# A two-layer encoder kernel: the expert tables multiplied as plain f32, and 96 of 256 tokens gathered instead of 32

## The reference

```python
def peer_ffn(h, w_q, sub_keys, u_tab, v_tab):
    q = rms_norm((hb @ w_q).reshape(PEER_BLOCK, PEER_HEADS, 2, PEER_D_KEY // 2))
    s = jnp.einsum('thpd,hpkd->thpk', q, sub_keys)            # 2 x 128 sub-keys per head
    v_top, i_top = lax.top_k(s, PEER_TOPK)                    # 16 best of each half
    best_s, best_pos = lax.top_k(cand_s, PEER_TOPK)           # 16 best pairs, 8 heads
    gate = jax.nn.softmax(best_s, axis=-1)
    u = jnp.take(u_tab, idx, axis=0)
    act = jax.nn.gelu(jnp.einsum('td,thkd->thk', hb, u))
    v = jnp.take(v_tab, idx, axis=0)
    return jnp.einsum('thk,thkd->td', gate * act, v)
```

## Time and profile before

| | |
|---|---|
| median of 3 runs | 1838.51 us (1835.72 to 1839.15) |
| profiled execution, first to last instruction (span) | 1830.5 us |
| around the span (median less span) | 8.0 us |
| PE busy | 1796.4 us, 98% |
| DVE busy | 1476.1 us, 81% |
| ACT busy | 1115.6 us, 61% |
| POOL busy | 769.2 us, 42% |
| moved by DMA | 391.70 MB, mean 214 GB/s |

### The profile page before, as it was taken

How to read it: one execution, slowest core, us unless ns; L and a number is a source line. 1 busy time by engine, 2 the same in 40 slices (tenths; PEclk the granted TensorE clock), 3 DMA queues, 4 the chain that set the end, 5 groups by cost and what they waited for, 6 DMA issues and landing times. The chain is left out here.

```text
span 1830.5 us, 38340 instructions
## 1 busy us (share of the span) xinstructions
PE 1796.4 (98%) x11836; PEld 1695.5 (93%) x11836; DVE 1476.1 (81%) x3273; ACT 1115.6 (61%) x2184; POOL 769.2 (42%) x452
## 2 busy tenths in 40 slices
PE   8999999999999999999999999999999999999998
PEld 6889999999999999999978899999999999999998
DVE  4765888988887888888667568889888878888886
ACT  5765566667776555555567555666677765555554
POOL 6545320037766444343064462100476755444430
PEclk9999999999999999999999999999999999999999
DMA  8232266664444899999512323666644448888884
GB/s 319 93 137 94 70 209 206 206 217 154 156 149 152 310 384 387 353 380 365 170 62 93 138 93 108 209 203 206 208 158 149 156 167 336 338 321 321 333 299 148
DMA packets 105485, 391.70 MB, mean 214 GB/s; under 512 B 12288, under 2 KB 16000, under 8 KB 102976
## 3 DMA queue, kind: packets, MB, share of 16 engines
q1 hardware_dynamic: 86336, 322.57, 50.6%
q0 software_dynamic: 19072, 68.23, 9.7%
HBM read 388.86 MB, written 1.05 MB: 213 GB/s over the span
## 5 line engine op out<-in xcount | busy, mean ns | idle before, releaser
L630 PE MATMUL ps<-fhl,wh 128*128 128x448 f32 (+1 forms) x2560 | 542.4, 356 | 4.3 <-DVE ps L1606 4.3
L630 PE MATMUL ps<-ghl,wh 128*128 128x448 f32 x2048 | 462.6, 367 | 1.7 <-DVE wl L1841 0.9
L630 PEld LDWEIGHTS ps<-fhl,wh 128*128 128x128 f32 x2560 | 429.7, 189 | 31.7 <-issue 3.4
L630 PEld LDWEIGHTS ps<-ghl,wh 128*128 128x128 f32 x2048 | 366.3, 189 | 26.3 <-issue 1.3
L1192 ACT ACTIVATE wh<-nat 128x1024 fp32r<-128x1024 f32 x260 | 275.7, 1060 | 177.2 <-PE ps L630 91.6
L1841 DVE TENSOR_TENSOR wl<-nat,wh 128x1024 fp32r<-128x1024 f32 x252 | 307.9, 1222 | 74.2 <-ACT wh L1320 73.7
L611 POOL TENSOR_TENSOR wl<-nat,wh 128x1024 fp32r<-128x1024 f32 x112 | 268.6, 2398 | 115.8 <-ACT wh L1192 115.8
L630 PEld LDWEIGHTS ps<-fhl,wl 128*128 128x128 f32 x2304 | 300.5, 191 | 9.0 <-POOL wl L580 1.0
L630 PE MATMUL ps<-fhl,wl 128*128 128x224 f32 (+1 forms) x2304 | 303.6, 274 | 0.6 <-POOL wl L580 0.6
L1319 ACT ACTIVATE ghl<-grid 128x224 fp32r (+1 forms) x252 | 98.6, 391 | 300.8 <-PE ps L630 287.0
L630 PEld LDWEIGHTS ps<-ghl,wl 128*128 128x128 f32 x2048 | 269.5, 191 | 6.5
(11 more groups left out here) (206 smaller groups left out, 2238.9 us busy)
## 6 DMA issues: line engine op xcount, KB each, us to landing
nat<-in_peer_u SPq DMA_DIRECT2D x256, 512.0 KB
nat<-in_peer_v SPq DMA_DIRECT2D x256, 512.0 KB
grid<-in_peer_wq SPq DMA_DIRECT2D x8, 2048.0 KB, 10.7
grid<-in_w_out SPq DMA_DIRECT2D x2, 4096.0 KB, 12.7
grid<-in_w_in SPq DMA_DIRECT2D x3, 2048.0 KB, 16.0
grid<-in_w_in SPq DMA_DIRECT2D x24, 256.0 KB
grid<-in_bias SPq DMA_DIRECT2D x2, 1664.0 KB, 16.8
grid<-in_w_in SPq DMA_DIRECT2D x2, 1024.0 KB, 23.5
```

What stands on the lines that cost most here:

```text
L630: return nc.tensor.matmul(dst, a, b, start=first, stop=last)
```

## The change

Three things change together.

- **No split in U and V.** `wh`, `wl`, `ghl` and all that makes them are gone from the two stages (they stay in the projections and queries). Each block is multiplied as it lands, plain f32, 8 products of 160 columns. `nat` is joined by `ring`, so that the stream has 8 slots; they are freed by PE itself (`prod_done`, `y_done`).
- **96 tokens gathered (NS = 96, DT = 160), one a partition.** A gather brings 96 rows of 4 KB, one pick of each of 96 tokens. That makes 128 gathers of U rows and 128 of V rows a layer, with 8 buffers. `dot` and `add_row` work on 96 partitions x 1024. The sums need no small product: DVE adds them to `x`.
- **Fewer gates.** 40 groups of four tokens, one beside every second block of the last 80 of U. ACT makes three of four `hota` by two steps each, DVE one.

```diff
-NS = 32
+OCT = 8
+NO = NK // OCT
+NS = 96
 DT = SEQ - NS
-NP = 4
-NPK = PH * TOPK // NP
-QS = (1, 15, 28)
-NB = DT // 4
+NPK = PH * TOPK
+GT = 4
+NG4 = DT // GT
+NB = 2 * NG4
 NA = NK - NB
+EARLY_DOTS = 24
...
-    for s in range(QUAD):
-        sp.wait_ge(rest_pool, past[rest_pool] + 2 * (NB + s - 1 - QUAD))
+    for s in range(OCT):
+        sp.wait_ge(prod_done, past[prod_done] + (NK - OCT + s + 1))
         fetch_v(0, s)
...
     def gather(m):
-        b, rows = m % 3, u_rows if m < NPK else v_rows
-        if m >= 3:
-            pool.wait_ge(gath_used, past[gath_used] + m - 2)
-        nc.gpsimd.indirect_dma_start(gath[b], None, rows, bass.IndirectOffsetOnAxis(
-            ap=picks[:, 1, m % NPK:m % NPK + 1].bitcast(U32), axis=0)).then_inc(gath_in[b], 16)
+        if m >= OCT:
+            pool.wait_ge(gath_used, past[gath_used] + m - OCT + 1)
+        nc.gpsimd.indirect_dma_start(gath[m % OCT][own, :], None, u_rows if m < NPK else v_rows, bass.IndirectOffsetOnAxis(
+            ap=lists[own, 3, m % NPK:m % NPK + 1].bitcast(U32), axis=0)).then_inc(gath_in[m % OCT], 16)
     pool.wait_ge(picked, past[picked] + 2)
...
+    for m in range(2 * NPK):
+        gather(m)
...
-    def product(q, s, rest, before):
-        pe.wait_ge(summed, past[summed] + count + 1)
-        pe.wait_ge(high_ready, past[high_ready] + count * 2 + 2)
+    def product(q, s):
+        pe.wait_ge(nat_in[s], past[nat_in[s]] + q * 16 + 16)
+        if not isinstance(q, int) or q * OCT + s >= 4:
+            pe.wait_ge(act_stored, past[act_stored] + q * OCT + (s - 3))
         for k in range(KD):
-            ins = mm(both, wh[:, b, k * P:(k + 1) * P], fhl[:, :, k, 0:DT], k == 0, False)
-        ins.then_inc(high_used, 1)
-        pe.wait_ge(rest, past[rest] + count * 2 + (2 - 2 * before))
-        for k in range(KD):
-            ins = mm(ps[:, 4 + b, 0:DT], wl[:, b, k * P:(k + 1) * P], fh[:, k, 0:DT], False, k == KD - 1)
+            ins = mm(ps[:, UBANKS[s % 4], 0:DT], slots[s][:, k * P:(k + 1) * P], xf[:, k, :], k == 0, k == KD - 1)
         ins.then_inc(prod_done, 1)
...
+    def late_oct(q):
+        for s in range(OCT):
+            product(q, s)
+            if s % 2 == 0:
+                gates(q - QA, s // 2)
...
     def block_v(q, s):
-        need_high(q, s)
-        for k in range(KD):
-            high_y(s % 2, k)
-        need_rest(q, s)
+        pe.wait_ge(nat_in[s], past[nat_in[s]] + q * 16 + 16 * (NO + 1))
         for k in range(KD):
-            ins = rest_y(s % 2, k)
+            ins = mm(block_y(k), slots[s][:, k * P:(k + 1) * P], at(grid8, q, s), first and k % 2 == 0, last and k % 2 == 1)
         ins.then_inc(y_done, 1)
...
+    def dot(n):
+        dve.wait_ge(gath_in[b], past[gath_in[b]] + 16 * (n // OCT + 1))
+        v.tensor_tensor_reduce(out=gath[b][own, :], in0=gath[b][own, :], in1=xs[own, :], scale=1.0, scalar=0.0,
+                               op0=ALU.mult, op1=ALU.add, accum_out=dots[own, n:n + 1]).then_inc(gath_used, 1)
+    for n in (*range(20), *range(31, 47), 64, 65, *range(20, 31), *range(47, 63)):
+        routing(n)
...
+    for m in range(NG4):
+        times_gates(m)
+        if m + 2 < NG4:
+            hots(m + 2)
+        for i in range(2):
+            dot(EARLY_DOTS + 2 * m + i)
+            times_gelu(NA + 2 * m + i, m + 1)
+    for n in range(EARLY_DOTS + 2 * NG4, NPK):
+        dot(n)
+    dve.wait_ge(acts_ready, past[acts_ready] + 1)
+    ch.step(v.tensor_tensor(amount[own, :], acts[own, :], lists[own, 0, 0:NPK], ALU.mult))
+    for n in range(NPK):
+        add_row(n)
+    dve.wait_ge(gath_used, past[gath_used] + 2 * NPK)
+    ch.step(v.tensor_tensor(x[own, 0, :], x[own, 0, :], acc[own, :], ALU.add))
```

More of the change, by code:

```diff
@@ L1323, in _ @@
-                    with act.Fori(1, QS[1]) as q:
-                        for s in range(QUAD):
-                            block_v(q, s)
+                    loop(act, 3, QA - 1, early_oct)
+                    act.wait_ge(lists_t, past[lists_t] + 1)
+                    A(ikt[:, :], ps[:, 6, 0:SEQ], ACT.Copy)
+                    A(jkt[:, :], ps[:, 6, SEQ:], ACT.Copy)
+                    A(nwkt[:, :], ps[:, 7, 0:SEQ], ACT.Copy, scale=-1.0)
+                    A(wkt[:, :], ps[:, 7, 0:SEQ], ACT.Copy).then_inc(listt_ready, 1)
@@ L1326, in _ @@
+                    act.wait_ge(listt_ready, past[listt_ready] + 1)
+                    for s in range(OCT):
+                        gelu(QA - 1, s)
+                        if s in (2, 5):
+                            hot_i(0, s // 3)
+                    late_oct(QA)
+                    loop(act, QA + 1, NO - 1, late_oct)
+                    late_oct(NO - 1)
                     act.wait_ge(gath_used, past[gath_used] + NPK)
-                    A(acts, dots, ACT.Gelu_apprx_tanh).then_inc(acts_ready, 1)
@@ L1328, in _ @@
-                    with act.Fori(QS[1], NQ) as q:
-                        for s in range(QUAD):
-                            block_v(q, s)
+                    A(acts[own, :], dots[own, :], ACT.Gelu_apprx_tanh).then_inc(acts_ready, 1)
                     if l == DEPTH - 1:
-                        low_sums(past[y_chunk], past[y_done])
+                        turn_y(past[y_chunk])
             @block.vector
@@ L1808, in quad_g @@
-                    def quad_g(g, first=False, last=False):
-                        for s in range(QUAD - last):
-                            if s:
-                                times_gelu(g, s - 1)
-                            elif not first:
-                                times_gelu(g, QUAD - 1, 1)
-                            add_halves(g + QA, s, half_b, s % 2)
-                            times_gates(g, s, first and s == 0)
-                            if not (last and s >= 2):
-                                hots(g + (s + 2) // QUAD, (s + 2) % QUAD, iota_ps)
@@ new lines, in _ @@
+                    for n in (*range(20), *range(31, 47), 64, 65, *range(20, 31), *range(47, 63)):
+                        routing(n)
+                    dve.wait_ge(picked, past[picked] + 2)
+                    for n in range(4):
+                        dot(n)
+                    routing(63)
+                    for n in range(4, EARLY_DOTS // 2 + 2):
+                        dot(n)
+                    ch.before()
+                    dve.wait_ge(listt_ready, past[listt_ready] + 1)
+                    hots(0)
@@ new lines, in _ @@
+                    hots(1)
+                    for n in range(EARLY_DOTS // 2 + 2, EARLY_DOTS):
+                        dot(n)
+                    dve.wait_ge(ones_ready, past[ones_ready] + late.shape[1])
+                    dve.wait_ge(act_stored, past[act_stored] + NA)
+                    for m in range(NG4):
[5 more added lines that the diff above has]
+                            times_gelu(NA + 2 * m + i, m + 1)
```

610 lines of the change are left out of this document (193 added, 417 removed).

## The result

The changed kernel takes **2105.7 us** (median of four runs, 2104.95 to 2123.99) where the kernel before, measured beside it, takes 1837.1 (1834.27 to 1839.15): a ratio of 1.1495, 95% interval 1.145 to 1.154. The forecast was 1740 and faster. It is 15% slower, and outside every case that the prediction listed.

What follows compares the result with a forecast made beforehand. PE was to bound U and DMA to bound V: 212.1 + 319 + 350 + 204.2 + 319 + 320 + 7.5 = 1731.8 us of span, with 8.0 to the median 1740 us. Its own range was 1715 to 1770, with rivals 1690 to 1843.

Steps and rivals of the forecast that it cites:

- the DMA term: Gathers and stream in U and V: at 386 GB/s U holds its pace, V is DMA-bound at 350 and 320 us.
- I take equal halves of 386: V: gathers and stream each get 193 GB/s, so the 144 gathers left take 293 us.
- 1.835 MB, 349 GB/s: under 386. So U holds its pace: Late part of U: two gathers and two blocks per 5.26 us of PE fit within the DMA rate.
- when 24 dots more (30 us) are done as well: U: gates begin at block 48, at 105 us, with 24 more dots by DVE already done.
- slower than before: Rival, V: only 12 engines carry 96-row gathers, 145 GB/s, 2.72 us each; 1858 us, 1.1% slower; 10% chance.
- the ports' case: Rival with 12% chance, most of it (10) counted as faster; its claim is not in the text given.
- the 84% for faster: Whole kernel: summed chance of a gain above 0.2% (3.7 us), from the forecast's 50% and parts of the rivals.
- a pass of 135 ns (136.5): PE in U and V: a 160-column pass takes 136.5 ns, so a block of 16 passes takes 2.18 us.
- DVE and POOL not the bound: DVE's group in U, 4.8 to 4.9 us, fits PE's 5.26; POOL costs nothing in V; POOL as bound 10%, 1820 us.
- both waiting for transfers in V: V: PE waits for transfers into `nat` and `ring`, about 0.5 us a block, and DVE waits for gathers.
- the border of 204: Between the layers, from V's end to the next U: left as it was, 204.2 us.
- a cost left out: V, where PE now pauses: a granted clock below 1 would cost time that the sum did not count.

Runs made afterwards that it cites:

- 1: Small kernel of transfers alone, encoder work left out: stream, gathers and plain transfers, alone or mixed; 96-row gathers 254 GB/s, 283 beside a 128-row stream.
- 6: Gathers alone, 16 KB rows, few kept of 128, 96 or 64 places, other work left out; fifth stretch: rows 0-3, 32 and 33 of 96, 27 GB/s.
- 3: Changed kernel with 128-row gathers, three for every four picks, the fourth pick reusing the third's rows, same gathered bytes: 1718.85 us, 0.936 of before.
- 7: Changed kernel with gathers of 128 places, every fourth skipped by an out-of-bounds index, tokens moved to the other partitions: 1735.0 us, 0.946 of before.
- 2: Changed kernel with all 128 rows in every gather, including rows nobody reads: 1819.53 us, 0.991 of before.

## Why the prediction was wrong

- **The step that failed:** the DMA term. "I take equal halves of 386" in V, and "1.835 MB, 349 GB/s: under 386. So U holds its pace" in U. The 386 came from stretches in which all transfers had 128 rows. A 96-row gather is another shape, and it does not only go slowly itself, it takes the stream's rate down with it: 283 GB/s in the mix (1), 272 to 309 in the kernel. The halves were right, the 386 was not. I carried a rate measured on one shape over to another, with a range of 375 to 400 around it.
- **The same terms with the measured rate.** V of layer 1: 144 gathers at 2.76 us are 397 us, and the last one is issued at 2048.3 us, 49 us before the end, in which the last gathers land and PE does the last 18 blocks. U of layer 1: the 80 blocks with gates need 1.835 MB per group, at 299 GB/s 6.1 us instead of 5.26, 35 us over 40 groups. The trace has them at 261 us instead of 214, so 12 us more. Here a second step failed, "when 24 dots more (30 us) are done as well": at the first of these blocks only 16 of the 24 were done, since VectorE waited for gathers, and 8 gathers (3.1 MB, 10 us at this rate) fell into the late part too. Behind these late dots PE also waited once for a one-hot (line 1594), 5 us a layer. The first 48 blocks took 110 us where 105 was forecast. The main part of the miss of U and of V has one cause.
- **The rivals.** In time "slower than before" (10%, 1858 us) came nearest, 248 us under the measurement. No run shows the term of the ports' case (12%, of which 10 are in the 84% for faster). In its place the runs showed that 96 rows laid evenly over both halves of the partitions are no faster (48 and 48 rows, 224 GB/s against 253), and that two engines with rows in 0-3, 32 and 33 together get the rate of one (27 GB/s, 6). That this is the whole price of a 96-row transfer is argued, not shown. No case had gathers and stream together as slow as 283 GB/s (1), so the range ended at 1843, 263 us under the measurement.
- **Right:** a pass of 135 ns (136.5); DVE and POOL not the bound; the equal halves, which no row of before showed (205 and 205 in 3; 142 and 147 in V of the changed kernel); both waiting for transfers in V; the border of 204. With the shape mended the time comes near the forecast of 1740, at 1719 (3) and 1735 (7), but partly by luck, since DMA moved 406 to 410 GB/s there and not 386: in 7 that offsets the turns lost to skipped places, and V of layer 1 is 284 us to its last product and a tail of 34, where 320 without a tail was forecast.
- **The clock.** It was granted at 0.77 in 640 to 700 with PE busy 38.8 of 60 us, and at 1.00 in 1800 to 1900 with 67.5 of 100. V is bound by gathers there, 2.63 us apart, so PE's slower passes were covered; I did not test that apart. The prediction had named this as a cost left out; with DMA mended little of it returns (mean clock 0.984 in 7 and 0.994 in 3, 0.965 after).
- **Slips in the sum, none of which decides it:** PE alone comes by the prediction's own terms to 1621 + 8 us, not 1590 + 8. With about 6 MB of weights the stream brings 104 blocks and not 102, and V of layer 0 is some 345 us, not 350. The 8.0 us around the span compare one execution's span with the median of others; in the profiled executions here time and span differ by 1.8 us.
- **Open:** how 64 and 112 rows are dealt (of 64 rows, 0 to 3 had packets of 1228 ns, while 0, 16, 32 and 48 had 611), and how much of the loss at 96 rows (254 GB/s against 389 to 399) is two engines slowing each other as in the fifth stretch of 6. The three parts of the change were not tried apart: what dropping the split gives with 32 gathered tokens no run shows.

## What to carry to other kernels

A DMA rate belongs to a shape: before you change how many partitions a transfer writes, measure the new shape alone and beside the stream, because a full DMA share says nothing of bytes (shares of 0.96 to 1.03 moved anything from 205 to 410 GB/s here). A transfer of 128 rows is worth keeping even where 32 of them are not wanted: skip them by an index out of bounds (297 GB/s alone against 255 for 96 rows), and spread the skipped places: every fourth took 1735.0 us, the last 32 1813.4. The skipped places still take turns, so beside another full queue they cost the gathers rate (174 against 205 GB/s). When the forecast hangs on one resource that the change loads in a way no row shows, its range must reach down to what the resource might give, and not only to how well the known rate was read.

## What the runs showed of the hardware

- Plain transfers of 4 KB rows alone, in GB/s: 128 rows 395 to 399, 120 rows 224, 112 rows 285, 96 rows 253 to 255, 80 rows 242, 64 rows 205; 64 rows on every second partition 370. Gathers alone: 128 rows 389 to 393, 120 rows 256, 112 rows 279, 96 rows 249 to 255, 64 rows 210 to 211. 120 rows are slower than 112 on either queue.
- With all transfers of 128 rows this core moved 409 to 410 GB/s over stretches of 100 us at a share of 1.03 (2, 3), above the 384 and 388 at 1.01 and 1.00; what held those back no run shows.
- Beside a 128-row stream, 96-row gathers slow the stream's packets as much as their own: medians of 231 and 232 ns in V of layer 1 of the changed kernel (1800 to 1900).
- A skipped place still leaves a small packet, with every fourth skipped: 33568 packets under 512 bytes where the changed kernel has 18208, a difference of 15360, the number of places skipped. They hardly lower the rate of both queues together (406 GB/s, where 3 has 410), but they count in their queue's turns: the gathers get 174 GB/s of it, where 3 has 205.
- Two full queues got equal numbers of packets though these differed in size: 6026 and 6026 in experiment 3 (586 to 686), 6374 and 6377 with every fourth place skipped (1555 to 1655).
